# ScalarE's negated copy of a weight unit, issued behind the high part of the unit ahead of it instead of before it

## The chip, the cores and the metric

The kernel runs on one core of one Trainium2 chip. The metric is the time of one execution on the device in microseconds (us). Three runs of the kernel before took 2129.9, 2131.62 and 2131.85 us; their median is 2131.62 us. All inputs are float32 in HBM, and 409 MB are read in one execution, nearly all of it weights.

## The reference

The model is two blocks over 256 tokens of width 2048.

```python
h = rms_norm(x, norm_mix);  proj = h @ w_in            # seven projections and two gates
y_a = hgrn2_mixer(...);     y_b = chunked_relpos_attention(...)
x = x + (gate_a * (y_a @ w_proj_a) + gate_b * (y_b @ w_proj_b)) @ w_out
h = rms_norm(x, norm_ffn)
ff_gate, ff_up = split(h @ w_ffn_in)                    # 2048 -> 2 x 5632
x = x + (silu(ff_gate) * ff_up) @ w_ffn_out             # 5632 -> 2048
# second block
h = rmsnorm(x, a_norm);  u, v, gate = split(h @ a_w_in) # 2048 -> 3 x 4096
u = gelu(u);  v = rmsnorm(gelu(v), v_gain)
y = u * (w_s mixing v over tokens + b_s)
x = x + (y * silu(gate)) @ a_w_out;  out = rmsnorm(x, final_norm)
```

Nearly all of the work is in these products of 256 tokens with large float32 weights.

## The kernel before, in words

**Split operands.** A float32 operand is written as a high part in the type fp32r (`w_hi`, `a_hi`, `ff_hi`) and a low part, the rest (`w_lo`, `a_lo`, `ff_lo`). A product is then three matmuls: high by high, the activation's low part by the weight's high part, and the activation's high part by the weight's low part.

**Units.** The weights pass through in units of 256 rows by 512 columns (512 KB). SyncE loads each into one of 8 slots of `raw` (line 580) and waits until the unit that had the slot is used. ScalarE makes the high part, `w_hi`, in one of 4 places (`RING`; `split`, line 734). VectorE makes `w_lo` as raw minus high, in place over `raw` (line 1324). TensorE then uses the unit and increments `unit_used`.

**The low part by DMA.** In four segments (`FFN_IN`, `FFN_OUT`, `V_IN`, `UG_IN`) some units get their low part in another way; there are 96 of them, in a step of 16 units mostly the units 3, 7, 11 and 15. For such a unit ScalarE writes minus the raw weights, rounded to fp32r, into one of two buffers `low` (line 741; rounding is the same with either sign, so this is minus the high part). GpSimd waits for that copy (`neg_ready`) and issues a DMA that adds the raw weights onto it (line 682); what lands is raw minus high. VectorE has nothing to do but a memset of one column that keeps the counting. TensorE does the eight matmuls with the high part first (line 2171), then waits for the DMA (`lo_added`) and does the four matmuls with `low` (line 2175).

**Order of ScalarE.** Its program is written out by hand. In a step over the units j of a segment, `ahead(k, i, j)` does the work for units that come later: `split` makes the high part of unit j+4, once TensorE has used unit j (the place is free then), and if unit j+5 is one with an added low part, its negated copy is made too. The copy waits only for the load of unit j+5. In `FFN_OUT` and `Y_FIRST`, `split` also makes the high part of two activation tiles (line 733) for every second unit. All added units have odd numbers, so the copies are made at even j. Behind `ahead` come, at odd j before a mixed pair, the copy of the weight sums `t_hi` (lines 869 and 870), at the end of a step the copies of the accumulated parts and the activation of the result (`parts`, `half_done`).

**Mixed pairs.** Some pairs of units are not multiplied in the plain way but with sums of weights and of activations (seven block products instead of eight). VectorE makes the sums of the raw weights (`t_sum`, lines 1544 to 1547), ScalarE their high part `t_hi` (line 870), VectorE their low part `t_lo` (line 1567), and TensorE uses them from line 2148.

The order of the work is set by program order on each engine and by semaphores alone; nothing plans it at run time.

Of the kernel before, what the change touches and what calls it, by code (L numbers as in the profile page):

```python
# [44 lines left out]
RING = 4  # L45
# [55 lines left out]
def build(nc, x, w_in, b_gate, norm_mix, norm_ffn, lb_logits, out_gain, q_gain, k_gain, rel_bias,  # L101
# [3 lines left out]
    with ctx:  # L105
# [368 lines left out]
        def tiles_ahead(k, i, j):  # L474

            ends_soon = isinstance(i, int) and i == S[k].steps - 1 and j >= S[k].pair - RING
            n = (j + RING) % S[k].pair
            if k == Y_LAST and not ends_soon:
                return Y_LAST, n % S[k].units * UK, j % RING
            if k == Y_FIRST and ends_soon:  # L480
                return Y_LAST, n * UK, j % RING
            if (k == Y_FIRST or k == UG_IN and ends_soon) and n % 2 == 0:
                return Y_FIRST, n // 2 * UK, n // 2 % PLACES
            if (k == FFN_OUT and not ends_soon or k == FFN_IN and ends_soon) and n % 2 == 0:
                return FFN_OUT, n // 2 * UK, place_of(i if k == FFN_OUT and j + RING == n else (i + 1) * (k == FFN_OUT), n // 2)
            return None

        def place_of(i, u):

            return (i * S[FFN_OUT].units + u) % PLACES  # L490
# [5 lines left out]
        def raw_slot(k, i, j):  # L496

            if isinstance(i, int):
                return after(k, i, j) % RAW
            assert S[k].pair % RAW == 0  # L500
            return (unit0[k] + j) % RAW

        def raw_use(k, i, j):

            if isinstance(i, int):
                return 16 * (after(k, i, j) // RAW + 1)
            return i * (16 * S[k].pair // RAW) + 16 * ((unit0[k] + j) // RAW + 1)
# [3 lines left out]
        def added_units(k, i):  # L511

            if k == FFN_OUT:
                return ADDED_OUT[i]
            if k == V_IN:
                return ADDED_V
            return tuple(unit for unit in ADDED if i or unit >= RING)
# [5 lines left out]
        def added(k, i, j):  # L523

            if k not in BY_DMA:
                return None
            one = isinstance(i, int)
            if j >= S[k].pair:
                if one and i == S[k].steps - 1:
                    return None  # L530
                i, j = i + 1, j - S[k].pair
            every = ADDED_V if k == V_IN else ADDED
            units = added_units(k, i) if one else every
            if j not in units:
                return None
            n = units.index(j)
            if one:
                c, i = added_from[k] + sum(len(added_units(k, q)) for q in range(i)) + n, 0
            else:
                c = added_from[k] + len(added_units(k, 0)) - len(every) + n  # L540
            return c % LOWS, i * (16 * len(every) // LOWS) + 16 * (c // LOWS + 1), n
# [3 lines left out]
        def after(k, i, units):  # L545

            return i * S[k].pair + (unit0[k] + units)
# [172 lines left out]
        def _(act):  # L720
            own = Chain(act, act_self)

            def split(slot, use, used, place, tiles=None):
                act.wait_ge(raw_in[slot], use)
                if used is not None:
                    act.wait_ge(unit_used, used)
                if tiles is not None:
                    k, t, at_ = tiles
                    if k == FFN_OUT:
                        act.wait_ge(tile_hi, TURN_FF + (t + 1) // 4 + 1)  # L730
                    else:
                        act.wait_ge(y_ready, (t + 1) // 4 + 1)
                    act.activation(S[k].operand[0][:, at_], (ff if k == FFN_OUT else y_all)[:, t:t + UK], ACT.Copy)
                act.activation(w_hi[:, place], raw[:, slot], ACT.Copy).then_inc(hi_ready, 1)  # L734

            def ahead(k, i, j):

                low_of = added(k, i, j + RING + 1)
                if low_of is not None:
                    act.wait_ge(raw_in[raw_slot(k, i, j + RING + 1)], raw_use(k, i, j + RING + 1))  # L740
                    act.activation(low[:, low_of[0]], raw[:, raw_slot(k, i, j + RING + 1)], ACT.Copy, scale=-1.0).then_inc(neg_ready, 1)  # L741
                split(raw_slot(k, i, j + RING), raw_use(k, i, j + RING), after(k, i, j + 1), j % RING, tiles_ahead(k, i, j))

            def step(k, i, evac, last=False, mid=None):

                s = S[k]
                for j in range(s.pair):
                    if not (last and j >= s.pair - RING):
                        ahead(k, i, j)
                    if j % s.units == s.units - 1 and not (last and j == s.pair - 1):  # L750
                        b = j // s.units
                        act.wait_ge(unit_used, after(k, i, j + 1))
                        evac(i, b)
                    if mid is not None:
                        mid(i, j)
# [103 lines left out]
            def double_ahead(k, i, j):  # L859

                n = coming(k, i, j)
                if n is not None and j % 2 == 1:
                    act.wait_ge(t_summed, pairs(k, i, n + 1))
                    ahead(k, i, j)
                    if not (isinstance(i, int) and pairs(k, i, n) == 0):
                        act.wait_ge(t_used, pairs(k, i, n))
                    if k in (FFN_OUT, Y_FIRST):
                        act.wait_ge(sf_summed, sums_made(k, i, n))
                        act.activation(sf_hi[:], sf_sum[:], ACT.Copy).then_inc(sf_hi_ready, 1)
                    act.activation(t_of(k)[1][:], t_of(k)[0][:], ACT.Copy).then_inc(t_hi_ready, 1)  # L870
                else:
                    ahead(k, i, j)
# [1712 lines left out]
```

## Time and profile before

| | |
|---|---|
| median of 3 runs | 2131.62 us |
| the profiled execution | 2129.97 us |
| its span in the profile | 2128.4 us |
| TensorE (PE) busy | 2117.2 us, 99% |
| VectorE (DVE) busy | 1749.9 us, 82% |
| ScalarE (ACT) busy | 1395.8 us, 66% |
| GpSimd (POOL) busy | 224.0 us, 11% |
| negated copies, line 741 | 96, mean 1046 ns |
| adding DMAs, line 682 | 96, 512 KB each, median 6.6 us from issue to landing |

The span begins with the first and ends with the last instruction that the profile counts; the execution's own time is 1.6 us longer. Busy shares are averages over all stages. Matmuls are pipelined: one of 512 columns is shown with 389 ns, but the next one starts 227 ns after it, so TensorE is fully used where matmuls start every 227 ns. Times in the rows are counted from the start of the span. In a row of the timeline, "x3" means that three instructions of a kind follow each other and are shown as one, and brackets give the idle time before it and what ended that.

### The profile page before, as it was taken

To read this page: it belongs to the slowest core of one execution; us is meant where nothing else is said; L and a number is where in the kernel's file an instruction comes from. 1 tells how busy PE (TensorE), PEld (TensorE's weight loads), DVE (VectorE), ACT (ScalarE), POOL (GpSimd) and SP (SyncE) were. 2 spreads that over 40 slices of the span, in tenths; PEclk is the share of its full clock that TensorE was granted. 3 is DMA by queue.
4 is the path that set the end of the run, shared out by engine and by line. 5 is a ranking of instruction groups with operands and counts; after the bars stand their busy time and mean duration, and the time that the engine had idled before them with its cause. 6 is when DMAs were issued, how large, how long until landed. Compare 5 with 4: busy or idle time off the path is not lost.

```text
span 2128.4 us, 30211 instructions
## 1 busy us (share of the span) xinstructions
PE 2117.2 (99%) x10098; PEld 1775.6 (83%) x10098; DVE 1749.9 (82%) x2295; ACT 1395.8 (66%) x1617; POOL 224.0 (11%) x314
## 2 busy tenths in 40 slices
PE   9999999999999999999999999999999999999998
PEld 9988888888888888888888888888888888888886
DVE  6578788676666699999899898988989999998976
ACT  6465455456545677766777677768778777877665
POOL 2021433201000000000000000000000111110000
PEclk9999999999999999999999999999999999999999
DMA  8666555676555689889998787877788888887664
GB/s 266 182 194 204 158 157 158 181 223 177 180 186 182 188 248 252 254 248 250 251 262 243 231 245 231 237 219 218 227 245 240 245 246 246 231 233 230 202 192 139
DMA packets 225344, 462.76 MB, mean 217 GB/s; under 512 B 14712, under 2 KB 14816, under 8 KB 225120
## 3 DMA queue, kind: packets, MB, share of 16 engines
q1 hardware_dynamic: 208608, 402.70, 59.5%
q0 software_dynamic: 15744, 55.65, 14.9%
q10 hardware_dynamic: 896, 3.15, 0.4%
q8 instruction: 57, 0.93, 0.2%
q14 instruction: 39, 0.32, 0.1%
HBM read 409.01 MB, written 3.16 MB: 194 GB/s over the span
## 4 chain that ended last, share of the span: by engine, by line
PE 98%; DVE 1%; ACT 0%; issue 0%; DMA 0%; DVEq 0%; SPq 0%; ACTq 0%
PE gp L2148 35%; PE gp L2080 33%; PE mx L2148 13%; PE gp L2171 8%; PE gp L2175 4%; PE mx L2428 1%; PE mx L2312 1%; PE mx L2477 1%; DMA x_tok<-x_in 0%; PE mx L2315 0%; PE mx L2309 0%; PE mx L2364 0%; PE mx L2408 0%; PE mx L2323 0%; PE mx L2352 0%
## 5 line engine op out<-in xcount | busy, mean ns | idle before, releaser
L734 ACT ACTIVATE w_hi<-raw 128x1024 fp32r<-128x1024 f32 x759 | 797.0, 1056 | 540.1 <-PE gp L2080 257.5
L1324 DVE TENSOR_TENSOR w_lo<-raw,w_hi 128x1024 fp32r<-128x1024 f32 x663 | 807.2, 1231 | 237.0 <-ACT w_hi L734 224.4
L2080 PE MATMUL gp<-w_hi,a_hi 128*128 128x512 f32 x576 | 230.0, 399 | 0.0
L2148 PE MATMUL gp<-w_hi,a_hi 128*128 128x512 f32 x585 | 228.0, 390 | 0.0
L2148 PE MATMUL gp<-w_lo,a_hi 128*128 128x512 f32 x585 | 227.7, 389 | 0.0
L2148 PE MATMUL gp<-w_hi,a_lo 128*128 128x512 f32 x585 | 227.6, 389 | 0.0
L2080 PE MATMUL gp<-w_lo,a_hi 128*128 128x512 f32 x576 | 224.6, 390 | 0.0
L2080 PE MATMUL gp<-w_hi,a_lo 128*128 128x512 f32 x576 | 224.3, 389 | 0.0
L682 POOL DMA_DIRECT2D low<-raw x96 | 81.2, 846 | 1228.8 <-ACT low L741 1228.8
L1567 DVE TENSOR_TENSOR t_lo<-t_sum,t_hi 128x1536 fp32r<-128x1536 f32 x102 | 178.8, 1753 | 10.1 <-ACT t_hi L870 7.1
L870 ACT ACTIVATE t_hi<-t_sum 128x1536 fp32r<-128x1536 f32 x102 | 150.8, 1479 | 4.7 <-PE gp L2148 4.7
L2148 PEld LDWEIGHTS gp<-w_lo,a_hi 128*128 128x128 f32 x585 | 109.8, 188 | 22.9
L2148 PEld LDWEIGHTS gp<-w_hi,a_hi 128*128 128x128 f32 x585 | 109.8, 188 | 22.8
L2148 PEld LDWEIGHTS gp<-w_hi,a_lo 128*128 128x128 f32 x585 | 109.8, 188 | 22.8
L2171 PE MATMUL gp<-w_hi,a_hi 128*128 128x512 f32 x328 | 128.2, 391 | 0.0
L2171 PE MATMUL gp<-w_hi,a_lo 128*128 128x512 f32 x328 | 127.6, 389 | 0.0
L2080 PEld LDWEIGHTS gp<-w_lo,a_hi 128*128 128x128 f32 x576 | 108.1, 188 | 23.2
L2080 PEld LDWEIGHTS gp<-w_hi,a_hi 128*128 128x128 f32 x576 | 108.2, 188 | 22.0 <-DVE w_lo L1324 0.4
L2080 PEld LDWEIGHTS gp<-w_hi,a_lo 128*128 128x128 f32 x576 | 108.3, 188 | 21.2
L2148 PE MATMUL gp<-w_hi,ff_hi 128*128 128x512 f32 x312 | 121.9, 391 | 0.0
L2148 PE MATMUL gp<-w_lo,ff_hi 128*128 128x512 f32 x312 | 121.4, 389 | 0.0
L2148 PE MATMUL gp<-w_hi,ff_lo 128*128 128x512 f32 x312 | 121.4, 389 | 0.0
(437 smaller groups left out, 4316.3 us busy)
## 6 DMA issues: line engine op xcount, KB each, us to landing
raw<-a_w_in_in SPq DMA_DIRECT2D x192, 512.0 KB, 5.1
raw<-w_ffn_in_in SPq DMA_DIRECT2D x176, 512.0 KB, 5.4
raw<-w_in_in SPq DMA_DIRECT2D x175, 512.0 KB, 3.7
low<-raw POOLq DMA_DIRECT2D x96, 512.0 KB, 6.6
raw<-w_ffn_out_in SPq DMA_DIRECT2D x88, 512.0 KB, 5.0
raw<-a_w_out_in SPq DMA_DIRECT2D x64, 512.0 KB, 4.6
raw<-w_out_in SPq DMA_DIRECT2D x32, 512.0 KB, 3.8
raw<-w_proj_a_in SPq DMA_DIRECT2D x16, 512.0 KB, 3.9
```

The source lines that it names most:

```text
L682: pool.dma_start(low[:, buf].bitcast(F32), raw[:, raw_slot(k, i, unit)], accum_op=ALU.add).then_inc(lo_added[buf], 16)
L734: act.activation(w_hi[:, place], raw[:, slot], ACT.Copy).then_inc(hi_ready, 1)
L870: act.activation(t_of(k)[1][:], t_of(k)[0][:], ACT.Copy).then_inc(t_hi_ready, 1)
L1324: dve.tensor_tensor(w_lo[:, slot], raw[:, slot], w_hi[:, place], ALU.subtract).then_inc(lo_ready, 1)
L1567: dve.tensor_tensor(t_of(k)[2][:], t_of(k)[0][:], t_of(k)[1][:].bitcast(F32), ALU.subtract).then_inc(t_lo_ready, 1)
L2080: ins = pe.matmul(out_, stat, mov, start=start, stop=last and p == 2, skip_group_check=True)
L2148: ins = pe.matmul(out_, stat[sp_], mov[mp], start=start and p == 0, stop=stop and p == 2, skip_group_check=True)
L2171: pe.matmul(gp[:, half, m], stat, w_hi[:, place, kk], start=start and q == 0, stop=False, skip_group_check=True)
L2175: ins = pe.matmul(gp[:, half, m], operand(k, i, u, kk, m)[0], low[:, buf, kk], start=False, stop=u == end and kk == UK - 1, skip_group_che ...
L2312: pe.matmul(part8[:, (l + 1) * P:(l + 2) * P], decay[buf][:, l, tb], decay[buf][:, l, tb], start=True, stop=True, skip_group_check=True)
L2428: ins = pe.transpose(turn_b[:, m, t * P:(t + 1) * P], src(t, m), ident[:])
L2477: ins = pe.matmul(mx[:, c // 2, t0:t0 + P], v_one[:, b, c * P:(c + 1) * P], ws_t[:, b, bass.ds(g, 1)].rearrange("p a n -> p (a n)"), start ...
```

## The change

In `ahead`, the call of `split` for unit j+4 moves from behind the negated copy of unit j+5 to before it. No instruction, wait, buffer or semaphore is added or removed; the DMA that GpSimd issues for the copy has the same wait as before.

```diff
             def ahead(k, i, j):
 
+                split(raw_slot(k, i, j + RING), raw_use(k, i, j + RING), after(k, i, j + 1), j % RING, tiles_ahead(k, i, j))
                 low_of = added(k, i, j + RING + 1)
                 if low_of is not None:
                     act.wait_ge(raw_in[raw_slot(k, i, j + RING + 1)], raw_use(k, i, j + RING + 1))
                     act.activation(low[:, low_of[0]], raw[:, raw_slot(k, i, j + RING + 1)], ACT.Copy, scale=-1.0).then_inc(neg_ready, 1)
-                split(raw_slot(k, i, j + RING), raw_use(k, i, j + RING), after(k, i, j + 1), j % RING, tiles_ahead(k, i, j))
```

## Rows read from the trace of the kernel before

**Rows 1.** The page's first part: busy us, share of the span, instructions.
```profile
PE 2117.2 (99%) x10098; PEld 1775.6 (83%) x10098; DVE 1749.9 (82%) x2295; ACT 1395.8 (66%) x1617; POOL 224.0 (11%) x314
```
**Rows 2.** Waits of PE in the whole span: waited for, us in total, times, longest.
```profile
PE mx L2112 <- DVE ones L1362: 1.3, 1, 1.3
PE mx L2148 <- DVE t_lo L1567: 0.6, 1, 0.6
PE gp L2080 <- DVE w_lo L1380: 0.5, 1, 0.5
PE gp L2080 <- DVE w_lo L1324: 0.4, 1, 0.4
```
**Rows 3.** All instructions of the tile low: durations in ns, minimum, median, maximum.
```profile
L741 ACT ACTIVATE low<-raw x96: 1037/1042/1091, 745.7 to 1929.0; 128x1024 fp32r<-128x1024 f32 x96
DMA to landing us min/median/max: 5.8/6.6/9.5
```
**Rows 4.** Timeline of ACT in FFN_IN: start, us, instruction.
```profile
912.08 1.04 ACT L741 ACTIVATE low<-raw 128x1024 fp32r<-128x1024 f32 x1
913.02 2.10 ACT L734 ACTIVATE w_hi<-raw 128x1024 fp32r<-128x1024 f32 x2
...
940.61 1.04 ACT L741 ACTIVATE low<-raw 128x1024 fp32r<-128x1024 f32 x1
941.94 1.06 ACT L734 ACTIVATE w_hi<-raw 128x1024 fp32r<-128x1024 f32 x1 [0.28 <-PE gp L2148]
```
**Rows 5.** The copy at 940.61: POOL's issue, its DMA, PE's first matmul with low.
```profile
L682 POOL DMA_DIRECT2D low<-raw x1: 847/847/847, 941.9 to 941.9; - x1
...
DMA to landing us min/median/max: 7.2/7.2/7.2
...
954.64 0.62 PE L2175 MATMUL gp<-low,a_hi 128*128 128x512 f32 x2
```
**Rows 6.** Timeline of ACT in FFN_OUT.
```profile
1252.35 1.48 ACT L870 ACTIVATE t_hi<-t_sum 128x1536 fp32r<-128x1536 f32 x1
1253.73 1.04 ACT L741 ACTIVATE low<-raw 128x1024 fp32r<-128x1024 f32 x1
1254.67 0.61 ACT L733 ACTIVATE ff_hi<-ff 128x512 fp32r<-128x512 f32 x1
1255.19 1.99 ACT L734 ACTIVATE w_hi<-raw 128x1024 fp32r<-128x1024 f32 x2
```
**Rows 7.** The copy at 1253.73: POOL's issue, its DMA, PE's first matmul with low.
```profile
L682 POOL DMA_DIRECT2D low<-raw x1: 845/845/845, 1255.1 to 1255.1; - x1
...
DMA to landing us min/median/max: 7.8/7.8/7.8
...
1263.63 0.62 PE L2175 MATMUL gp<-low,ff_hi 128*128 128x512 f32 x2
```
**Rows 8.** The copy at 1278.85: the same three.
```profile
L682 POOL DMA_DIRECT2D low<-raw x1: 842/842/842, 1280.2 to 1280.2; - x1
...
DMA to landing us min/median/max: 8.0/8.0/8.0
...
1289.47 0.62 PE L2175 MATMUL gp<-low,ff_hi 128*128 128x512 f32 x2
```
**Rows 9.** FFN_OUT (1195 to 1412 us): POOL's issues for low and their DMAs.
```profile
L682 POOL DMA_DIRECT2D low<-raw x14: 832/842/850, 1217.3 to 1396.8; - x14
...
DMA to landing us min/median/max: 5.8/7.7/9.5
```
**Rows 10.** V_IN's first step: timelines of ACT, DVE and PE.
```profile
1463.24 1.05 ACT L741 ACTIVATE low<-raw 128x1024 fp32r<-128x1024 f32 x1
1464.19 2.94 ACT L734 ACTIVATE w_hi<-raw 128x1024 fp32r<-128x1024 f32 x3
...
1465.27 1.23 DVE L1324 TENSOR_TENSOR w_lo<-raw,w_hi 128x1024 fp32r<-128x1024 f32 x1 [1.75 <-ACT w_hi L734]
...
1476.49 1.75 DVE L1567 TENSOR_TENSOR t_lo<-t_sum,t_hi 128x1536 fp32r<-128x1536 f32 x1
...
1477.30 0.39 PE L2148 MATMUL gp<-w_lo,s_hi 128*128 128x512 f32 x1
1478.30 0.50 PE L2148 MATMUL mx<-t_hi,s_hi 128*128 128x512 f32 x1 [0.61 <-DVE t_lo L1567]
```

## The prediction

> **What bounds the kernel now.** I read the page's busy shares first. TensorE is busy for 2117.2 of 2128.4 us [rows 1], so at most 11.2 us of the span could be won by anything. Then I read whom TensorE waits for. In the whole execution five waits are listed, four of them here, and three of the four stand in the first stages, where no low part is added by DMA [rows 2]. The one in the segments that the diff touches is 0.6 us long, on `t_lo`. TensorE is never shown waiting for an added low part. So the stretch from 745 to 1945 us, in which the 96 copies stand [rows 3], is gapless but for that one place. The question is then not what ScalarE saves, but how much earlier than TensorE needs it each added part lands, and whether the later copy still makes it. For that I followed single copies: ScalarE's timeline, GpSimd's issue, the landing, and the first matmul with `low`.
>
> **The change, part by part.** Nothing is added or removed; two items of ScalarE's program swap. There are 96 swaps.
>
> *The split moves ahead.* Where ScalarE is behind, the high part of unit j+4 comes earlier by one copy: at 912.08 the copy starts, the next instruction at 913.02, so 0.94 us [rows 4]. Where ScalarE is not behind, the split waits for TensorE anyway: at 940.61 the copy starts, and the split at 941.94 after 0.28 us of idle time that PE ends [rows 4]. There it gains nothing.
>
> *The copy moves back.* Where ScalarE is behind in FFN_IN, V_IN and UG_IN, the delay is one split, 0.95 us (913.02 minus 912.08, and the two splits have nearly the same length). Where the split waits, the copy now waits with it: it starts at 941.94 + 0.95 = 942.89 instead of 940.61, 2.3 us later. In FFN_OUT the split before an added unit always has the activation tiles with it: from the copy's 1253.73, `ff_hi` starts 0.94 us on, `w_hi` another 0.52 us on [rows 6]. The group `ff_hi` plus `w_hi` takes 0.52 + 0.95 = 1.47 us, which is the delay there.
>
> *The slack.* The copy at 940.61 is issued as a DMA at 941.9, lands 7.2 us later at 949.1, and is first needed at 954.64 [rows 5]: 5.5 us of slack against a delay of 2.3. I went through all 43 of FFN_IN in this way; the slack is 2.1 to 6.0 us, where it is small the delay is only 0.95, and at least 1.1 us is left everywhere. V_IN (8) and UG_IN (31) look the same, with at least 1.1 us left. FFN_OUT is tighter, since its adds take 7.7 us in the median and 9.5 at most [rows 9] against 6.6 over all [rows 3], and their delay is longer. The copy at 1253.73 is issued at 1255.1, lands at 1262.9, and is needed at 1263.63 [rows 7]: slack 0.8, delay 1.47, so TensorE waits 0.7 us. The one at 1278.85 is issued at 1280.2, lands at 1288.2, is needed at 1289.47 [rows 8]: slack 1.3, so 0.2 us. Three more of the 14 have a slack of 1.5 to 1.8 us and just make it by this sum. If a wait that is resolved less than 0.3 us ahead already costs, which is my assumption, the 14 cost 2.0 us instead of 0.9. I take the middle, **1.5 us lost in FFN_OUT**. From below this term is 0 (the delayed DMA meets less traffic and takes the 5.8 us of the fastest one [rows 9]). From above, if each took the 9.5 us of the slowest, ten of the fourteen would be late by 11.4 us together.
>
> *A rule on this.* The adds take 5.8 to 9.5 us for 512 KB [rows 3]. The Trainium skill ("DMA: Bandwidth & Descriptors", section "Anatomy of one DMA — SWDGE (gpsimd) path") gives a transfer of this path about 2.0 us plus its bytes over 436 GB/s; as an estimate by that page, 3.2 us. By that figure every add would land over 4 us earlier than in the rows, the loss in FFN_OUT would be nil, and the sum would come out below the time before. The trace does not agree (other loads share the engines here), so the sum goes by the rows. The same page ("Rules for kernel authors") says to issue a DMA early and to wait for it late, and the change does the contrary; what that costs is the term above.
>
> *The one wait on `t_lo`.* In V_IN's first step the copy at 1463.24 stands before three splits, and VectorE had been idle for 1.75 us when the first of them let its `w_lo` go at 1465.27 [rows 10]. From there VectorE works almost without a break to `t_lo` at 1476.49, which ends at 1478.24. TensorE's last matmul before the sums starts at 1477.30 and the next could follow 0.23 us later, but starts at 1478.30: 0.77 us lost [rows 10]. With the split first, VectorE's chain starts 0.95 us earlier, and `t_lo` ends at 1477.3. **Gain 0.75 us**; from below 0, if a wait in the chain keeps its time; above 0.77 there is nothing to win.
>
> *What else is passed.* `t_hi` comes at odd j, with a split on either side of the even j between, so it is not pushed back by the copy: by the time the next split may start, 2.7 us after the last (twelve matmuls at 227 ns), split and copy of 1.9 us are through. At the end of a step the copy now sits between the split and the activation of the result; where ScalarE waited for TensorE that delays the activation by 0.3 us, beside work of VectorE, and TensorE is gapless there. GpSimd has nothing behind its wait for the copy but the next issue (and in UG_IN a copy of `v_one`, made a step ahead). SyncE's loads wait for `unit_used` and don't move. I take 0 for all of these; from above, 17 step ends by 0.3 us are 5 us if nothing hid them, which the gapless TensorE speaks against.
>
> *Sum.* The profiled execution took 2129.97 us, span 2128.4. It becomes 2129.97 + 1.5 - 0.75 = 2130.7 us. That execution is 1.65 us under the median of the runs; on the median the same sum is 2131.62 + 0.75 = **2132.4 us**.
>
> **The rivals.**
> *A, slower: the adds of FFN_OUT land late as a rule.* One mechanism: an add that starts 1.47 us later runs beside one more weight load, and takes as long as the slowest there. For it: the segment's adds spread from 5.8 to 9.5 us, so timing against the loads matters. Against it: the median is 7.7, and the delay shifts by only half a unit's time. It decides once the adds of the segment take about 8.7 us, one more than now: worked out for all 14 with their issue and need, 8.0 us each would cost 1.2 us, 8.7 us 4.1 us, 9.0 us 6.5 us. Price: up to 11.4 us, 2142 us; at 9.0 us each 2131.62 + 6.5 - 0.75 = 2137 us.
> *B, faster: V_IN's wait goes and the adds all make it.* Then 2131.62 - 0.75 = 2130.9 us. For it: the loss in FFN_OUT rests on two adds of 14. More than this there isn't to win between 745 and 1945 us.
> *C, the change does nothing to the path*: waits in VectorE's chain keep `t_lo` where it is, adds fit: 2131.6 us.
>
> **How the numbers follow.** My forecast (a loss in FFN_OUT of 0.5 to 3 us, half given back) gets 0.55, B 0.17, C 0.16, A 0.12. Runs of this kernel lie within 2 us of each other, so 0.2%, 4.3 us, is about what can be told from no change. Only A from adds of 9 us on goes beyond that, and nothing on the winning side does. Faster by over 0.2%: 0.02. Slower by over 0.2%: 0.09. Within: 0.89. The range goes from 2129.8 (B, and the lowest run) to 2136.5 (A begun).
>
> **What would show it right or wrong.** In the profile after, the waits of TensorE should list one on the DMA into `low` in FFN_OUT, of 1 to 2 us in total, in one to five places, the one near 1263 first. The wait on `t_lo` near 1478 should be gone. Copies behind a waiting split should start 2.3 us later, those behind a ready one 0.95 or 1.47 us. VectorE's waits for `w_hi` should shrink without effect. I am wrong if TensorE waits for `low` in FFN_IN or UG_IN, if its waits there pass 4 us, or if the time falls by more than 1 us with TensorE's busy rows unchanged.

## The result

The changed kernel takes 2137.89 us (median of 7 runs, 2136.5 to 2140.96); the kernel before, run beside it, 2130.24 us (7 runs, 2129.9 to 2131.85). The ratio is 1.0035, 95% interval 1.0026 to 1.0045: 7.65 us slower, clear of the 4.3 us that I took as the bound. I had forecast 2132.4 us and a range up to 2136.5. The forecast stood on the median of the three runs that were there at the time, 2131.62 us; as a change it was 0.75 us slower, and 7.65 were measured. Three runs far off the rest (4179.99 and 3802.55 us of the kernel before, 2945.49 us of the kernel with the half delay, below) are in no ratio, and nothing here explains them.

The profiled execution of the changed kernel took 2140.96 us, the longest of the seven, with a span of 2139.4 us. The page's busy line, against [rows 1], shows 2.4 us more of "busy" time on TensorE; the rest of the 11.0 us is time in which it stood still:

```profile
span 2139.4 us, 30211 instructions
...
PE 2119.6 (99%) x10098; PEld 1776.5 (83%) x10098; DVE 1750.4 (82%) x2295; ACT 1396.4 (65%) x1617; POOL 219.4 (10%) x314
```

Whom TensorE waits for, after. The columns are those of [rows 2]. The wait on `t_lo` of 0.6 us is gone; `y_one`, the adding DMA and `s_lo` are new. The line "issue" is the sixth wait of the same kind as the five for `y_one`, 0.84 us at 1912.78, for which the profile names no releaser:

```profile
PE mx L2148 <- ACT y_one L1244: 4.4, 5, 0.9
PE gp L2175 <- DMA low<-raw: 3.4, 2, 2.4
PE mx L2112 <- DVE ones L1362: 1.3, 1, 1.3
PE mx L2148 <- issue: 0.8, 1, 0.8
PE mx L2428 <- DVE s_lo L1844: 0.5, 1, 0.5
```

Times of the same instruction in both traces, a landmark, say where the 11.0 us of this execution (2140.96 against 2129.97 us) went. I take the first matmul with `low` of each of the 96 units, and list how far the later trace is behind, wherever that changes much:

```
stage     unit first needed at (before)   behind by     what changed there
FFN_IN    757 to 1194 us                  -0.1          nothing
FFN_OUT   1289.47                         +2.45         wait for an add
FFN_OUT   1305.11                         +4.21         TensorE slow after that wait
FFN_OUT   1334.33                         +4.76         wait for s_lo
FFN_OUT   1355.42, 1371.06                +6.09         wait for an add
V_IN      1505.41                         +5.27         wait for t_lo gone: -0.83
UG_IN     1692.74                         +6.23         +0.96
UG_IN     1736.44, 1780.13, 1823.82,
          1867.52, 1911.18                +11.00        +0.95 each
```

So FFN_OUT gave 6.1 us in this execution, V_IN gave 0.8 back, and UG_IN took 5.7, in six steps of one size.

**FFN_OUT.** ScalarE's timeline at the place of [rows 8], before and after. Before, the copy starts 1.38 us behind `t_hi`. After, `ff_hi` and `w_hi` come between, and it starts 2.85 us behind it, 1.47 more. `t_hi` itself is 1.04 us later too, since ScalarE waits ahead of it for VectorE's `t_sum`, which came later. So the copy comes 2.51 us later in all:

```profile
1277.47 1.48 ACT L870 ACTIVATE t_hi<-t_sum 128x1536 fp32r<-128x1536 f32 x1
1278.85 1.04 ACT L741 ACTIVATE low<-raw 128x1024 fp32r<-128x1024 f32 x1
```

```profile
1278.51 1.48 ACT L870 ACTIVATE t_hi<-t_sum 128x1536 fp32r<-128x1536 f32 x1
1279.89 0.61 ACT L733 ACTIVATE ff_hi<-ff 128x512 fp32r<-128x512 f32 x1
1280.41 1.04 ACT L734 ACTIVATE w_hi<-raw 128x1024 fp32r<-128x1024 f32 x1
1281.36 1.04 ACT L742 ACTIVATE low<-raw 128x1024 fp32r<-128x1024 f32 x1
```

Its add, from GpSimd's instruction to its landing, took 9.2 us, where it had taken 8.0 before, and TensorE waited:

```profile
L682 POOL DMA_DIRECT2D low<-raw x1: 842/842/842, 1282.7 to 1282.7; - x1
...
DMA to landing us min/median/max: 9.2/9.2/9.2
```

```profile
1289.16 0.39 PE L2171 MATMUL gp<-w_hi,ff_lo 128*128 128x512 f32 x1
1291.92 2.07 PE L2175 MATMUL gp<-low,ff_hi 128*128 128x512 f32 x4 [2.38 <-DMA low<-raw]
1293.79 0.63 PE L2148 MATMUL mx<-w_hi,ff_hi 128*128 128x512 f32 x1
1294.22 0.63 PE L2148 MATMUL mx<-w_hi,ff_lo 128*128 128x512 f32 x1
```

**UG_IN.** ScalarE at the end of a step, before and after, at the same place of the program (the step that ends near 1683 us before). Before, the copy stands in time in which ScalarE had nothing to do (0.28 us of it are left over); after, it stands between the split and all that follows:

```profile
1676.70 1.06 ACT L741 ACTIVATE low<-raw 128x1024 fp32r<-128x1024 f32 x1
1678.05 1.06 ACT L734 ACTIVATE w_hi<-raw 128x1024 fp32r<-128x1024 f32 x1 [0.28 <-PE gp L2148]
1679.12 1.28 ACT L1233 ACT_TABLE_LOAD   x1
1680.42 1.34 ACT L1233 ACTIVATE c_part<-c_part,small 128x512 f32<-128x512 f32 x2
1681.66 1.54 ACT L1244 ACTIVATE y_one<-mx,vec 128x256 f32<-128x256 f32 x4
```

```profile
1683.31 1.06 ACT L734 ACTIVATE w_hi<-raw 128x1024 fp32r<-128x1024 f32 x1 [1.28 <-PE gp L2148]
1684.27 1.04 ACT L742 ACTIVATE low<-raw 128x1024 fp32r<-128x1024 f32 x1
1685.33 1.28 ACT L1233 ACT_TABLE_LOAD   x1
1686.63 1.34 ACT L1233 ACTIVATE c_part<-c_part,small 128x512 f32<-128x512 f32 x2
1687.87 1.54 ACT L1244 ACTIVATE y_one<-mx,vec 128x256 f32<-128x256 f32 x4
```

From the start of `w_hi` to the start of `y_one` it is 3.61 us before and 4.56 after: 0.95 more. `y_one` is what ScalarE reads out of the accumulator `mx`, and TensorE may not write there for its next step before this is done (`sv_copied`). Before, `y_one` ended at 1683.20 and TensorE's matmul started at 1683.34. After, it ends at 1689.41, the matmul starts at 1689.55, and the trace shows a wait:

```profile
1682.75 0.60 PE L2428 MATMUL mx<-ident,wide 128*128 128x128 f32 x4
1683.34 0.49 PE L2148 MATMUL mx<-w_hi,a_hi 128*128 128x512 f32 x1
```

```profile
1689.55 0.49 PE L2148 MATMUL mx<-w_hi,a_hi 128*128 128x512 f32 x1 [0.94 <-ACT y_one L1244]
```

In all six steps the distance from the end of `y_one` to this matmul is 0.10 to 0.14 us, the same before and after. So the 0.14 us are the handing over and no room: TensorE was already held by `y_one` before the change, and a delay of 0.95 us cost 0.95 us each time. The list of waits hides this, because the matmuls of 128 columns ahead of it are shown with 272 ns and start every 109 ns. The last of them started at 1683.08 and the next matmul 0.26 us later; where `y_one` was ready in good time (the kernel `all_sv` below), that distance is 0.03 us.

### The profile page after: what moved, and what is told of

It reads as the page before. It is cut to its first block, busy times and chain, and to the rows that moved or that the text cites. A ratio compares the mean times of both kernels' runs of the same rounds, so it can differ in the third digit from the quotient of the medians.

```text
span 2139.4 us, 30211 instructions
## 1 busy us (share of the span) xinstructions
PE 2119.6 (99%) x10098; PEld 1776.5 (83%) x10098; DVE 1750.4 (82%) x2295; ACT 1396.4 (65%) x1617; POOL 219.4 (10%) x314
## 4 chain that ended last, share of the span: by engine, by line
PE 96%; ACT 2%; DMA 1%; DVE 0%; issue 0%; ACTq 0%; DVEq 0%; SPq 0%
PE gp L2148 34%; PE gp L2080 33%; PE mx L2148 13%; PE gp L2171 7%; PE gp L2175 4%; PE mx L2428 1%; PE mx L2312 1%; DMA low<-raw 1%; PE mx L2477 1%; ACT y_one L1244 0%; ACT L1233 0%; DMA x_tok<-x_in 0%; PE mx L2315 0%; ACT low L742 0%; ACT w_hi L734 0%
```

## The experiments

Each kernel is the kernel before with the order changed only where a condition holds. The short diff is the same for most of them, and the condition is given with each:

```diff
             def ahead(k, i, j):
 
+                behind = CONDITION
+                if behind:
+                    split(...)
                 low_of = added(k, i, j + RING + 1)
                 ...
-                split(...)
+                if not behind:
+                    split(...)
```

All ran in five rounds beside the kernel before. The medians of the latter were 2130.24 to 2130.51 us; where I give a difference it is against the median of the same group of runs. Line numbers in these kernels are 4 higher behind `ahead` (7 in the kernel with the half delay).

**Where in UG_IN.** Three kernels: the whole of UG_IN, only its last place (j = 14), and all but that.

```diff
+                behind = k == UG_IN
```

> The order is changed in UG_IN alone. The profile after showed TensorE waiting for y_one (line 1244) at the head of six UG_IN steps, 0.95 us each, while the adds there landed in time. Theory 1 (the copy, made ahead of the half-step activation and of y_one, pushes y_one past TensorE's need): 2130.2 + 5.7 = 2135.9 us, ratio 1.0027, six waits of 0.9 us, none for low. Rival (the UG_IN waits are only passed on from the late FFN_OUT stage, with its shifted loads): ratio 1.0000.

```diff
+                behind = k == UG_IN and j == S[k].pair - 2
```

> The order is changed in UG_IN at j = 14 alone, where the copy is of unit 3 of the next step. Theory 1: this place carries the whole UG_IN loss, 2135.9 us, ratio 1.0027. Rival (later adds of units 7, 11 and 15 press on TensorE or on the DMA queues): 2130.2 us, ratio 1.0000.

```diff
+                behind = k == UG_IN and j != S[k].pair - 2
```

> The order is changed in UG_IN at j = 2, 6 and 10, not at 14. Theory 1: nothing, ratio 1.0000 within 0.0005, no wait for y_one and none for low. Rival (later adds of units 7, 11, 15): ratio up to 1.0027.

Measured: UG_IN whole 2135.86 us, ratio 1.0026 (1.0016 to 1.0037). The place at j = 14 alone 2135.86 us, 1.0025 (1.0015 to 1.0035). So the one place carries all of it, 5.6 us, as theory 1 had it. But all places except this one cost 2134.75 us, 1.0021 (1.0012 to 1.0030), where I had expected nothing. The waits of TensorE in that kernel, columns as above:

```profile
PE mx L2152 <- ACT y_one L1248: 2.5, 3, 1.0
```

The same wait, though the copy was in its old place. ScalarE's timeline shows why: the copy itself now waited for the load of its weights.

```profile
1763.14 1.50 ACT L874 ACTIVATE t_hi<-t_sum 128x1536 fp32r<-128x1536 f32 x1
1765.68 1.06 ACT L744 ACTIVATE low<-raw 128x1024 fp32r<-128x1024 f32 x1 [1.04 <-DMA raw<-a_w_in_in]
1766.64 1.04 ACT L734 ACTIVATE w_hi<-raw 128x1024 fp32r<-128x1024 f32 x1
```

That load is the first of three that SyncE issues there. Issue to landing of the three, before and in this kernel:

```profile
L580 SPq DMA_DIRECT2D raw<-a_w_in_in x3: 372/372/372, 1758.1 to 1760.8; - x3
...
DMA to landing us min/median/max: 5.7/5.8/5.8
```

```profile
L580 SPq DMA_DIRECT2D raw<-a_w_in_in x3: 373/373/743, 1758.5 to 1761.2; - x3
...
DMA to landing us min/median/max: 7.1/7.1/7.2
```

The first landed at 1763.83 before and the copy started at 1764.10; the room was 0.28 us. Now it took 7.14 us. Step by step the loads of this kernel took 6.3, 6.6, 7.1, 7.4, 7.3 and 6.9 us, and TensorE's idle time at `y_one` was 0, 0.15, 0.70, 0.97, 0.87 and 0.44 us. The DMA engines are 97 to 98% busy in this stretch in both kernels; that the later adds take their share from these loads is argued from this.

**Which of the later adds.** Four kernels:

```diff
+                behind = k == UG_IN and j == 10
```

> The order is changed in UG_IN at j = 10 alone (the copy of unit 15, whose add then starts 2.2 us later). In the kernel with j = 2, 6 and 10 changed, the copy at j = 14 stood where it was but waited about 1 us for its weight load, which shared the DMA engines with the later add of unit 15, and y_one came late again. Theory 2 (the later add of unit 15 slows the load of unit 3 of the next step): all of that loss is here, 2130.3 + 4.4 = 2134.7 us. Rival (a shift of every later add in the step is needed): below 2131.5 us.

```diff
+                behind = k == UG_IN and j in (2, 6)
```

> Order changed in UG_IN at j = 2 and 6 (units 7 and 11), not at 10 and 14. Changing j = 10 alone cost nothing though the load of unit 3 of the next step then took 6.2 us, against 5.75 us before and 7.1 us with all three changed; the copy at j = 14 has 0.3 us between that load's landing and its start and the split behind it another 0.3 us of idle time. Theory 3 (the three later adds add up in the nearly full DMA engines, and only together push the load past that room): 2130.3 to 2131.5 us. Rival (units 7 and 11 carry it): 2134.7 us.

```diff
+                behind = k == UG_IN and j in (6, 10)
```

> Order changed in UG_IN at j = 6 and 10 (units 11 and 15). Theory 3: the load of unit 3 of the next step takes between 6.2 and 7.1 us, so that part of the 4.4 us appears: 2131.0 to 2133.5 us. Rival (unit 7's add is what matters, or all or nothing): 2130.3 us.

```diff
+                behind = k == UG_IN and j in (2, 10)
```

> Order changed in UG_IN at j = 2 and 10 (units 7 and 15). With 6 and 10 changed the load of unit 3 of the next step took 7.1 to 7.7 us, with 2 and 6 6.0 to 6.5 us, with 10 alone 6.2 us. Theory 5 (the add of unit 11, later, runs into the loads that the add of unit 15, later, then finds unfinished; unit 7's has been worked off by then): 6.3 us load, 2130.3 to 2131.0 us. Rival (any two later adds sum up): 2134 to 2135 us.

```
places changed      time of that load in five or six steps     median, us   against before
none (before)       5.5 to 6.0                                 -            -
10                  6.2 (once 4.2)                             2130.15      -0.1
2 and 10            6.2 (once 4.6)                             2130.61      +0.1
2 and 6             6.0 to 6.5                                 2130.83      +0.5
2, 6 and 10         6.3 to 7.4                                 2134.75      +4.4
6 and 10            7.1 to 7.7                                 2135.38      +5.0
```

Theory 2, the add of unit 15 alone, fell: that kernel is level with before (0.9999, 0.9990 to 1.0008). Theory 3, a plain sum of three, fell too: it had put 6 with 10 at 2131.0 to 2133.5 us, but these two cost no less than all three, and 2 with 10 cost nothing (1.0000, 0.9991 to 1.0009). Theory 5 stands: the later adds of units 11 and 15 must both be there (6 and 10: 1.0022, 1.0013 to 1.0031). The time follows the load's time, not the number of changes: up to about 6.3 us it fits into the room (the 0.28 us before the copy and 0.28 us of idle time behind it), and past that the rest is paid, in five steps with 2, 6 and 10 changed and in all six with 6 and 10. That a queue of unfinished transfers is handed on from the one add to the other is my reading of the load times; I have not shown the queue itself.

**Taking the wait's cause away.** If all of this comes through `y_one`, it must go when `y_one` gets room. At j = 14 these two kernels make `y_one` ahead of the activation of the half step:

```diff
-                    sooner = k == UG_IN and j == S[k].pair - 1
+                    sooner = k == UG_IN and j >= S[k].pair - 2
                     if sooner:
                         mid(i, j)
```

once with UG_IN changed at 2, 6 and 10, and once with the whole change.

> Order changed in UG_IN at j = 2, 6, 10; beside it, at j = 14 y_one (line 1244) is made ahead of the activation of the half step. Theory 2 (the loss comes only through y_one being late): y_one has about 2.6 us of room now and the loss of 4.4 us goes, 2130.3 us. Rival (slow loads delay TensorE in another way too): stays above 2133 us.

> The whole change, and y_one made ahead of the activation of the half step in UG_IN. Theory 1: the 5.7 us of UG_IN go; what stays is FFN_OUT's 2.6 us less V_IN's 0.85: 2132.0 us, no waits for y_one. Rival (once y_one is off, the next thing behind it on ScalarE, w_turned or t_hi, is late instead): 2134 us or more.

Measured: 2131.44 us, ratio 1.0005 (0.9996 to 1.0014), where 2134.75 stood without the edit; and 2132.77 us, 1.0012 (1.0003 to 1.0021), where 2137.89 stood. The whole change thus loses 5.1 of its 7.65 us by giving ScalarE's `y_one` room, without moving one negated copy. In the second, TensorE's waits list no `y_one` any more, but what was left over:

```profile
PE gp L2179 <- DMA low<-raw: 1.0, 1, 1.0
...
PE mx L2432 <- DVE s_lo L1848: 0.5, 1, 0.5
```

Both kernels stay 0.8 to 1.1 us above my figure, and the traces show where. At the matmul behind `y_one` TensorE now gains 0.1 to 0.2 us in each of the six steps, since it isn't held there any more:

```profile
1683.60 0.60 PE L2432 MATMUL mx<-ident,wide 128*128 128x128 f32 x4
1683.96 0.47 PE L2152 MATMUL mx<-w_hi,a_hi 128*128 128x512 f32 x1
```

Some 3 us later it loses 0.2 to 0.4 us. There it waits for the copy `wide` (line 1251, 1255 here), which ended 1.1 us before it was needed in the kernel before and now ends 0.05 us (in the last step 0.15) before TensorE goes on:

```profile
1773.50 1.01 ACT L1255 ACTIVATE wide<-mx 128x1024 f32<-128x1024 f32 x1
```

```profile
1774.56 0.50 PE L2152 MATMUL mx<-t_hi,s_hi 128*128 128x512 f32 x1
```

This is the rival that I had named for `all_sv` (`wide` is its `w_turned`), at a small price: with the gain at `y_one` counted in, 0.8 to 0.9 us over the six steps. It seems to be the price of moving `y_one`, since it is paid as well in the fifth step of the first kernel, where the load took 4.2 us and the copy was on time. The kernel before with that edit alone was not run.

**FFN_OUT.** First whole, then with the copy between `ff_hi` and `w_hi`, later by 0.52 us instead of 1.47:

```diff
+                behind = k == FFN_OUT
```

> The order is changed in FFN_OUT alone, where each copy comes 1.47 us later behind ff_hi and w_hi. Theory 1: TensorE waits for adds into low in this segment, one to five places; what is left of the measured 7.6 us after 5.7 of UG_IN and the 0.85 gained in V_IN is 2.8 us, so 2133.0 us, ratio 1.0013, with a spread over runs of some us since the adds take 5 to 9 us. Rival (the adds make it in a typical run and the 6 us of the profile after were an accident of it): ratio 1.0000 to 1.0003.

```diff
             def split(slot, use, used, place, tiles=None, between=None):
                 ...
                     act.activation(S[k].operand[0][:, at_], ...)
+                if between is not None:
+                    between()
                 act.activation(w_hi[:, place], raw[:, slot], ACT.Copy).then_inc(hi_ready, 1)
```

> Order of before everywhere but in FFN_OUT, where the copy comes between ff_hi and w_hi: 0.52 us later than before, instead of 1.47. Theory (each add has its own room, the loss is what is missing of it): by the adds' room in the profile before (0.76, 1.26, 1.48, 1.59 us and more) none is missed in a typical run, loss 0 to 0.5 us, 2130.3 to 2130.8 us. Rival (any delay there costs in proportion): a third of 2.6 us, 2131.2 us.

Measured: 2132.88 us, ratio 1.0013 (1.0004 to 1.0022), so 2.6 us; its eleven runs go from 2131.5 to 2134.0, while the kernel before keeps within half a microsecond in most of its runs. A landing time that changes from run to run, against a fixed need, would give just that; only one run of each kernel was traced. The half delay gives 2131.25 us, 1.0003 (0.9994 to 1.0012): 0.9 us by the medians. Theory (0 to 0.5) and rival (0.9) seemed to be decided for the rival, but the trace says otherwise. The adds cost 0.25 us in it, at one place (the one needed first at 1355.42 before); the largest loss, 0.56 us, is this one, where TensorE turns the rows of the next operand:

```profile
1332.12 1.09 PE L2435 MATMUL mx<-ident,wide 128*128 128x128 f32 x8 [0.54 <-DVE s_lo L1851]
```

Before, the turn started at 1331.55, 0.14 us later than the matmul ahead of it allowed and 0.06 us behind the end of `s_lo`: here too TensorE was held already. ScalarE's `a_hi` (line 1091), `a_two`, and then `s_hi` stand behind the copy at j = 2 of the second step, 0.55 us later in this kernel (1322.32 against 1321.77), and VectorE's `s_lo` behind them. Two kernels take this place apart from the thirteen others:

```diff
+                behind = k == FFN_OUT and i == 1 and j == 2
```

> Order changed at one place of FFN_OUT alone: second step, j = 2, where the copies of the next operand (a_hi, a_two, then s_hi) stand behind it on ScalarE. With the half delay TensorE waited 0.54 us for s_lo at its turn near 1332 us. Theory 4 (the same displacement as of y_one): 0.5 us at that turn, shown as a wait for s_lo, no wait for an add; 2130.8 us. Rival (the s_lo wait comes from the later adds of the first step): no such wait, 2130.3 us.

```diff
+                behind = k == FFN_OUT and not (i == 1 and j == 2)
```

> Order changed at the other 13 places of FFN_OUT. Theory 4: no wait for s_lo; only the waits for adds of the kernel with FFN_OUT changed whole, so its 2132.9 less 0.5: 2132.4 us. Rival (the adds cost nothing by themselves): 2130.3 us.

Measured: the one place 2130.84 us, ratio 1.0002 (0.9993 to 1.0011), too little to be told by the runs, but its waits list `s_lo` with 0.5 us and no add, and from that place on its trace is 0.6 us behind. The others 2132.44 us, 1.0012 (1.0003 to 1.0021), with a wait for an add of 1.2 us and none for `s_lo`:

```profile
PE gp L2179 <- DMA low<-raw: 1.2, 1, 1.2
```

So FFN_OUT's 2.6 us are, by the medians, some 2 us of late adds, and by the traces 0.5 us of a displaced operand.

**FFN_IN and V_IN alone.**

```diff
+                behind = k == FFN_IN
```

> Order changed in FFN_IN alone, 43 adds. The profile after has every add there in time (0.9 us in hand at the least) and FFN_IN ending at the same time as before. Theory: nothing, 2130.3 us, ratio 1.0000. Rival (it gives something that the profile hides, as a clock step or late loads): outside 2129.8 to 2131.5 us.

```diff
+                behind = k == V_IN
```

> The order is changed in V_IN alone. Theory: the wait of TensorE for t_lo near 1478 us goes, nothing else: 2130.3 - 0.85 = 2129.5 us, ratio 0.9996, which may be under what runs can tell; the profile should show no wait for t_lo there. Rival (the wait went because FFN_OUT's stall shifted things): the wait of 0.6 us stays and the ratio is 1.0000.

FFN_IN: 2130.45 us, ratio 0.9999 (0.9990 to 1.0008); 43 later adds, nothing. V_IN: 2129.20 us, 0.9995 (0.9986 to 1.0004). Its trace has no wait for `t_lo` and is 0.96 us ahead from there to the next landmark, and the runs' medians differ by 1.0 us. No other kernel here has a median more than 0.1 us below that of the kernel before. The trace says why, but the interval includes 1, so the runs alone don't show a gain. As a version to use it is the whole change without FFN_IN, FFN_OUT and UG_IN.

## Why the prediction was wrong

**The step that failed** is "What else is passed": "At the end of a step the copy now sits between the split and the activation of the result; where ScalarE waited for TensorE that delays the activation by 0.3 us, beside work of VectorE, and TensorE is gapless there. ... I take 0 for all of these". Two things in it were wrong.

The size: the copy takes 0.95 us of ScalarE's time. Before, it lay in a wait that would otherwise have been idle (0.95 + 0.28 us of it, [rows 4] show the like in FFN_IN). Behind the split it covers nothing, so all that follows comes 0.95 us later. I had looked at the activation in FFN_IN, which waits for VectorE itself (0.58 us at 943.58) and so loses only part, 0.3 us in the profile after too, and carried that to UG_IN.

The cover: I took a gapless TensorE as proof that there was room. In the list of waits it looked gapless, but `y_one` was already the last thing it waited for, in every one of the six steps, and there was no room at all. I had measured the room of the adds, one by one, and of nothing else. The isolated place (`ug_end`'s 5.6 us, all that UG_IN costs) shows that this term alone is 5.6 of the 7.65 us. It was not among the rivals: A, the slow one, was put in FFN_OUT with slower adds.

A bound was there: I wrote that the step ends could cost 5 us if nothing hid them, and then left it out of the range. With it the range would have gone to 2137.4, still below the 2137.89 measured. That it came so near is luck: it was 17 step ends by 0.3 us, and what was paid were six by 0.95.

**FFN_OUT, forecast 1.5 us, measured 2.6** (`ffn_out_only`). The mechanism was right: an add that starts later is late at few places, one wait of 0.9 to 1.2 us in most profiles. The term missed the wait for `s_lo`, 0.5 us, which is the failed step again in another place. The places were off: the wait I put first, near 1263 us, is listed in no profile. The one at 1355, with 1.59 us of room, which I had down as just in time, was in each with all or nearly all of FFN_OUT changed, and 1289 in the profile after alone. The step behind this is the delay of 1.47 us that I took for all 14. It holds where all else on ScalarE stands still. But VectorE's sums came at other times, and ScalarE's `t_hi` with them: against TensorE, the copy of 1263 came 0.2 us earlier, that of 1289 came 2.4 us later in the profile after and 0.5 us with FFN_OUT alone, that of 1355 came 1.7 us later.

**Rival A** asked for adds that take 8.7 us or more on average. They took 7.2 us on average in the profile after and 7.4 with FFN_OUT alone, against 7.6 before. Single ones of 9.2 us came [rows 9 show 9.5 before], but the later start did not make them slower as a rule. A's price was near the measured time by accident.

**V_IN, forecast 0.75 gained, 0.83 in the profile after and 0.96 in `v_in_only`'s.** Right, chain and size; that more than 0.77 us could not be won was wrong, since the matmuls beside the wait follow each other faster too. Delays of the copies of 0.95 and 2.3 us: right for most of FFN_IN, while in V_IN and UG_IN they were 0.6 to 2.3 us. No waits for adds in FFN_IN or UG_IN: right but for 0.2 and 0.1 us in the two kernels with UG_IN changed at 2, 6 and 10. In V_IN, where I had at least 1.1 us left, one add of the profile after landed 0.04 us before its use at 1479.90 and cost 0.2 us.

**The skill's rule.** By "DMA: Bandwidth & Descriptors" of the Trainium skill, section "Anatomy of one DMA — SWDGE (gpsimd) path", an add would take 3.2 us as an estimate, and none would ever be late. In all profiles here adds take 4.7 us and more. I also wrote that every add would land over 4 us earlier by that figure; against [rows 3] it is 2.6 to 6.3 us, 3.4 in the median, which changes nothing in the sum. Its advice in "Rules for kernel authors", to issue early and wait late, agrees with what FFN_OUT measured.

**A second cost that no part of the prediction had**: three adds made later in UG_IN slow the load that the copy at j = 14 waits for by 1.4 us. I had written that SyncE's loads don't move; they are issued at the same place of the program, but land later. In the changed kernel this is hidden, since the copy there stands behind the split and the load still lands 0.8 to 1.1 us before it starts. That is why UG_IN whole costs no more than its last place, although the other places cost 4.4 us by themselves.

## What to carry to other kernels

An instruction that lies in an idle wait costs nothing; moved behind the wait's end it costs its whole length to everything behind it in program order, so list those instructions and their consumers before the moved one's own. A busy engine without listed waits says nothing of the room behind it: measure, for each thing that it consumes, how long before the need it was ready (here 0.8 to 8 us for the adds, and nothing for `y_one`), and whether the engine's instructions start as closely there as elsewhere. When two costs are priced from different places, test each place alone: here 5.6 and 4.4 us of one stage together made 5.6.

## What the runs showed of the hardware

In the profile after, TensorE stood still for 2.4 us for an add. The following matmuls of 512 columns started 427 ns after one another instead of 227, and the granted clock of that stretch, the third number from the end of its row, was 0.52, which is the lower of the two levels (1.2 of 2.4 GHz); then it was 1.00 again:

```profile
1280.00:1292.00 12.00, 9.62 (x44) 7.64 (x42) 11.83 (x18) 9.07 (x11) 0.84 (x1) 1.00 0.82 235
1292.00:1295.50 3.50, 3.50 (x9) 2.78 (x10) 3.04 (x4) 1.23 (x2) 0.00 (x0) 0.52 0.11 31
1295.50:1300.00 4.50, 4.50 (x21) 3.70 (x20) 3.05 (x4) 3.84 (x6) 0.45 (x1) 1.00 0.76 251
```

The landmark table shows its price: 2.45 us for the wait, 1.76 more by the next landmark. The waits of 0.5 to 1.3 us in all the profiles brought no such stretch; a lower clock stands nowhere else in them but in the last microseconds of each execution. There is only one wait of this length, so that it brought the lower clock is likely and not shown. The same lines show that the DMA engines fell to 11% there: the loads wait for TensorE's units, so a stop of TensorE stops them too.
